# A hybrid decoder trunk: the decay gaps of the state space stage as one VectorE difference, clipped on ScalarE

## The reference, cut to what matters

```python
def step(state, inp):                      # one chunk, c = 128
    ...
    acum = jnp.cumsum(dtc * a.astype(jnp.float32), axis=1)
    diff = acum[:, :, None] - acum[:, None]            # (i, j, head)
    seg = jnp.exp(jnp.where(mask, diff, -jnp.inf))     # mask: j <= i
    xdt = xc * dtc[..., None]
    scores = jnp.einsum('bihn,bjhn->bijh', cc, bc) * seg
    y_intra = jnp.einsum('bijh,bjhp->bihp', scores, xdt)
    y_inter = jnp.einsum('bihn,bhpn->bihp', cc * jnp.exp(acum)[..., None], state)
    a_last = acum[:, -1]
    w = jnp.exp(a_last[:, None] - acum)[..., None]
    state = state * jnp.exp(a_last)[..., None, None] + jnp.einsum('bjhn,bjhp->bhpn', bc * w, xdt)
    return state, y_intra + y_inter
```

## Time and profile before

| | |
|---|---|
| median of 3 runs | 2202.1 us (2201.56 to 2203.22) |
| the profiled execution: its time | 2200.59 us |
| its span in the trace | 2198.8 us, so 1.8 us lie around the span |
| PE busy | 2137.9 us (97%) |
| DVE busy | 1230.1 us (56%) |
| ACT busy | 723.9 us (33%) |
| convolution stretch | 638 to 704 us in the span |
| chunk loop | 707 to 785 us in the span |

### The profile page before, as it was taken

How to read it: one execution, slowest core, us unless ns; L and a number is a source line. 1 busy time by engine, 2 the same in 40 slices (tenths; PEclk the granted TensorE clock), 3 DMA queues, 4 the chain that set the end, 5 groups by cost and what they waited for, 6 DMA issues and landing times.

```text
span 2198.8 us, 27851 instructions
## 1 busy us (share of the span) xinstructions
PE 2137.9 (97%) x10057; PEld 1738.0 (79%) x10057; DVE 1230.1 (56%) x1983; ACT 723.9 (33%) x1001; POOL 53.0 (2%) x94
## 2 busy tenths in 40 slices
PE   8999999999999989999999999999997999999998
PEld 7888888788787778888888888888755678888886
DVE  6535346586548986444356444445578545435344
ACT  4222224344325543222224222223355643222222
POOL 0000000000000000000000000000002300000000
PEclk9999999999999999999999999999998999999999
DMA  6333434322153324444443333333210013333321
GB/s 172 98 97 96 108 86 106 86 59 59 50 132 96 87 58 115 107 112 106 115 106 105 96 104 93 99 96 86 86 51 11 1 48 96 96 95 95 100 80 69
DMA packets 356347, 195.61 MB, mean 89 GB/s; under 512 B 13635, under 2 KB 348614, under 8 KB 356262
## 3 DMA queue, kind: packets, MB, share of 16 engines
q1 hardware_dynamic: 353622, 184.73, 29.7%
q0 software_dynamic: 2640, 9.77, 2.7%
HBM read 191.55 MB, written 2.79 MB: 88 GB/s over the span
## 4 chain that ended last, share of the span: by engine, by line
PE 86%; DVE 9%; issue 2%; ACT 2%; DMA 1%; POOL 0%; SPq 0%; DVEq 0%; ACTq 0%
PE ps L1435 25%; PE ps L1436 25%; PE ps L1437 25%; PE ps L1619 1%; PE ps L1904 1%; PE ps L1892 1%; DVE w_lo L786 1%; DVE index_scores L1318 1%; PE ps L1454 1%; PE ps L1455 1%; PE ps L1456 1%; PE ps L1636 1%; PE ps L1634 1%; PE ps L1635 1%; DVE index_scores L1303 1%
## 5 line engine op out<-in xcount | busy, mean ns | idle before, releaser
L467 ACT ACTIVATE w_hi<-w_raw 128x1024 fp32r<-128x1024 f32 x351 | 371.8, 1060 | 1067.6 <-PE ps L1437 994.7
L1435 PE MATMUL ps<-h_hi,w_hi 128*128 128x512 f32 x1640 | 641.4, 391 | 0.0
L1436 PE MATMUL ps<-h_lo,w_hi 128*128 128x512 f32 x1640 | 639.0, 390 | 0.0
L1437 PE MATMUL ps<-h_hi,w_lo 128*128 128x512 f32 x1640 | 638.9, 390 | 0.0
L786 DVE TENSOR_TENSOR w_lo<-w_raw,w_hi 128x1024 fp32r<-128x1024 f32 x351 | 429.0, 1222 | 290.5 <-ACT w_hi L467 290.4
L1435 PEld LDWEIGHTS ps<-h_hi,w_hi 128*128 128x128 f32 x1640 | 308.4, 188 | 66.0 <-issue 2.2
L1437 PEld LDWEIGHTS ps<-h_hi,w_lo 128*128 128x128 f32 x1640 | 308.4, 188 | 63.9
L1436 PEld LDWEIGHTS ps<-h_lo,w_hi 128*128 128x128 f32 x1640 | 308.5, 188 | 63.6
L1435 PE MATMUL ps<-act_hi,w_hi 128*128 128x512 f32 x704 | 274.0, 389 | 0.0
L1437 PE MATMUL ps<-act_hi,w_lo 128*128 128x512 f32 x704 | 273.9, 389 | 0.0
L1436 PE MATMUL ps<-act_lo,w_hi 128*128 128x512 f32 x704 | 273.9, 389 | 0.0
(11 more groups left out here) (301 smaller groups left out, 2086.3 us busy)
## 6 DMA issues: line engine op xcount, KB each, us to landing
w_raw<-in_ffn_w_gate SPq DMA_DIRECT2D x88, 512.0 KB, 3.8
w_raw<-in_ffn_w_up SPq DMA_DIRECT2D x88, 512.0 KB, 3.8
w_raw<-in_ffn_w_down SPq DMA_DIRECT2D x64, 512.0 KB, 3.9
w_raw<-in_hy_w_in SPq DMA_DIRECT2D x44, 512.0 KB, 3.8
w_raw<-in_ffn_w_down SPq DMA_DIRECT2D x32, 384.0 KB, 3.3
w_raw<-in_hy_w_out SPq DMA_DIRECT2D x16, 512.0 KB, 4.0
acum_rows<-acum_scratch POOLq DMA_DIRECT2D x4, 1024.0 KB, 9.9
bias_rows<-line_scratch POOLq DMA_DIRECT2D x8, 512.0 KB, 6.8
```

Source lines behind the costliest of these rows:

```text
L467: act.activation(w_hi[:, s, :], w_raw[:, s, :], ACT.Copy).then_inc(hi_ready, 1)
L1435: pe.matmul(ps[:, bank, :], wh, rh[:, k, :], start=k == 0, stop=False)
L1436: pe.matmul(ps[:, bank, :], wh, rl[:, k, :], start=False, stop=False)
L1437: mm = pe.matmul(ps[:, bank, :], wl, rh[:, k, :], start=False, stop=k == nk - 1)
```

## The change

DVE's 16 instructions of `gaps` become one TENSOR_TENSOR over 128 x 2048 elements, with the sign turned (`acum_j - acum_i`) and without the bound. ACT gets one more instruction over the same 128 x 2048, a Relu in place, which bounds the differences at zero from below, and a wait for it; the exponential then takes a scale of -1. Nothing else is changed.

```diff
@@ ACT, decays(c)
                     act.wait_ge(s_D, c + 1)
-                    act.activation(ssd_attn[:, c % 2, :, :], ssd_attn[:, c % 2, :, :], ACT.Exp).then_inc(s_pexp, 1)
+                    act.activation(ssd_attn[:, c % 2, :, :], ssd_attn[:, c % 2, :, :], ACT.Relu).then_inc(s_clip, 1)
+                    act.wait_ge(s_clip, c + 1)
+                    act.activation(ssd_attn[:, c % 2, :, :], ssd_attn[:, c % 2, :, :], ACT.Exp, scale=-1.0).then_inc(s_pexp, 1)
                     act.wait_ge(s_wd, c + 1)
@@ DVE, gaps(c)
-                    for h in range(SH):
-                        ins = dve.tensor_scalar(ssd_attn[:, c % 2, h, :], acum_chunk[:, h, :], acum_tok[:, c, h:h + 1], 0.0, ALU.subtract, ALU.min)
-                    ins.then_inc(s_D, 1)
+                    dve.tensor_tensor(ssd_attn[:, c % 2, :, :], acum_tok[:, c, :].rearrange("p (h o) -> p h o", o=1).to_broadcast([P, SH, P]),
+                                      acum_chunk, ALU.subtract).then_inc(s_D, 1)
```

More of the change, by code:

```diff
@@ L266, in build_program @@
         s_conv, s_conved, s_silu, s_pad = sem("s_conv"), sem("s_conved"), sem("s_silu"), sem("s_pad")
-        s_ea, s_pexp, s_wd, s_w, s_D, s_P, s_C = (sem(n) for n in ("s_ea", "s_pexp", "s_wd", "s_w", "s_D", "s_P", "s_C"))
+        s_ea, s_clip, s_pexp, s_wd, s_w, s_D, s_P, s_C = (sem(n) for n in ("s_ea", "s_clip", "s_pexp", "s_wd", "s_w", "s_D", "s_P", "s_C"))
         s_cbm, s_tr, s_trB, s_Bev, s_xdt, s_xdtw = (sem(n) for n in ("s_cbm", "s_tr", "s_trB", "s_Bev", "s_xdt", "s_xdtw"))
```

## The result

The changed kernel takes 2208.4 us (median of 20 runs, 2200.35 to 2211.84) against 2201.85 us before (20 runs, 2196.85 to 2203.54). The ratio is 1.0027, 95% interval 1.002 to 1.0034: slower by 0.2 to 0.34%. The profiled execution took 2207.52 us, its span is 2205.7.

What follows compares the result with a forecast made beforehand. DVE's chain through the last convolution tile and chunk loop was taken to bound the kernel, with PE behind it; 5.04 + 0.58 = +5.62 us gave a median of 2207.7 us, range 2206.7 to 2208.9, wider 2204.5 to 2210.5.

Steps and rivals of the forecast that it cites:

- DVE's gain: In gaps, one 2.28 us instruction replaces 16 taking 3.75, 3.23 and 3.22 us: 1.47, 0.95 and 0.94 us gained.
- ACT's price: Relu of 1.91 us before the exponential, table load no longer hidden: 3.23 us from Relu's start to exponential's start.
- The piece: From start of gaps to start of from_start, chunks 0 to 2: 9.66 us each, ACT the bound, together +5.04 us.
- the 2.58 us to spare on DVE: DVE's slack against ACT within each 9.66 us stretch from gaps to from_start, claimed for all three chunks.
- The convolution stretch: Before the chunk loop, the Relu beside chunk 0's decays makes the last convolution tile late by 0.58 us.
- The 0.29 us: Shorter gaps(0) lets DVE start the tile of m = 8 at 682.02, not 682.31, so ACT's following work starts earlier.
- Sum: Chunk loop 5.04 plus last convolution tile 0.58 us: +5.62 us, median from 2202.1 to 2207.7, +0.26%.
- The load doesn't hide: Rival, chance 0.10: the load hides behind the Relu, each of three pieces loses 1.30 us, leaving +1.7 us, not slower.
- part of the delay was swallowed: Rival, chance 0.16: engine hand-overs hide part, or the last tile's 0.58 is absent; +3.5 to +4.1 us, not slower.
- A dearer switch: Rival, chance 0.06 together with a dearer Relu: an undetected pipeline drain adds 1.3 us a piece, +9.6 us, 2211.7.
- PE's clock did fall: Rival, chance 0.06: PE's clock falls behind the longer wait for chunk 1's xdtw, adding 0 to 2 us, up to 2209.7.
- the 3.71: PE's forecast wait in us for xdtw of chunk 1: 1.96 before, with 1.75 more.

Runs made afterwards that it cites:

- e3: Changed kernel without the Relu, exponential scaled by -1/1024 (output not the reference's), so the DVE half alone: stretch -3.32 us against before, ratio 0.9989.
- e2: Kernel before, its 16 small DVE instructions kept, with only the Relu and the exponential of scale -1 added on ACT: stretch +8.75 us, ratio 1.0047.
- e1: Changed kernel plus a 128 x 1 exponential ahead of ACT's wait for the gaps, loading the set early: stretch +2.08 us against before, ratio 1.0013.
- e10: Changed kernel run again unaltered, with its trace: stretch 89.51 us, +5.62 against before, ratio 1.0027.
- e4: Changed kernel with ACT's exponentials for from_start and xdtw first, Relu and gaps' exponential last: stretch -3.28 us against before, ratio 0.9978.
- e7: Changed kernel with Relu and gaps' exponential last, and chunk 0's pair moved to just ahead of the chunk loop: stretch -4.63 us against before, ratio 0.9978.

## Why the prediction was right

**DVE's gain.** Forecast 2.28 us for the one difference; it took 2.28 to 2.29 in all four places, and e3 shows the gain alone, 1.47, 0.93 and 0.93 us. That the 1.47 comes out whole took the 3.75 us of the earlier trace rows, of which 0.53 is the long instruction of e2's section.

**ACT's price.** Forecast 1.91 for the Relu, 3.23 with the load; it took 1.90 to 1.94 and 3.21 to 3.25. That the load lies on the path was the larger point: e1 takes 3.57 us away by moving it ahead of the wait.

**The piece.** Forecast 9.66 in all three chunks, measured 9.66, 9.68, 9.67, so +5.07 where +5.04 was said. One reading in it was wrong without touching the sum: the 2.58 us to spare on DVE hold for chunks 1 and 2 (0.54 for PE and 1.89 for ACT, and 2.50). In chunk 0 DVE has 5.56, since its own work there was not 8.02 but 7.91 - 2.34 = 5.57 us before and is 4.1 now.

**The convolution stretch.** Forecast +0.58, measured +0.57. The 0.29 us that the shorter `gaps(0)` gives back are in it too: in e2, which lacks them, the tile is 0.86 late.

**Sum.** +5.62 forecast, +5.65 and +5.62 measured in the stretch. The medians moved by 6.55 us; for the changed kernel 2207.7 was forecast and 2208.4 measured. The further 0.9 us are not resolved: the stretch repeats to 0.03, the rest of an execution doesn't (816.1 to 819.3 us for one kernel in the part that e10 looks at), and the interval of the ratio (4.4 to 7.5 us) takes in both.

**The rivals.** The load doesn't hide: it starts 0.01 us after the Relu's end. No part of the delay was swallowed. A dearer switch isn't there: 1.31 us from the Relu's end to the exponential's start. PE's clock did fall, as that rival had it, but its price was nothing. PE's timeline in the changed kernel has 3.03 us of idle time ahead of chunk 1's `xdtw` matmuls, the first of which is in the earlier trace rows:

```profile
734.25 3.55 PE L1738 MATMUL ps<-xdtw,ssd_B 128*128 128x512 f32 x4 [3.03 <-DVE xdtw L1165]
```

The four took 1.95 us before, and the busy time by stretch shows the granted clock at about half, near 1.2 GHz, while they ran:

```profile
734.00:736.00 2.00, 1.75 (x2) 0.84 (x3) 2.00 (x3) 0.00 (x0) 0.00 (x0) 0.52 0.12 35
736.00:738.00 2.00, 2.00 (x7) 0.60 (x7) 2.00 (x2) 0.00 (x0) 0.00 (x0) 0.63 0.04 8
```

DVE waited 0.54 us for PE's outputs, and then still 1.89 for ACT: the late outputs used up DVE's spare time and no more. In e10 it came closer: 1.69 us for PE's outputs and then 0.72 for ACT, with the same piece of 9.67. So that this costs nothing is shown for two executions, with a margin of 0.72 us in one of them. The clock fell in a second place that the prediction doesn't name: the late tile makes PE wait 2.24 us for the last silu, ahead of the loop, instead of 1.68, and from 708 to 710 us the granted clock is 0.50 where it was 1.00. From the last tile to the first `gaps` of the loop DVE still takes 16.74 us in both kernels. The wait was 3.03 us and not the 3.71 that I worked out, since PE was done with the gate unit ahead of it only at 731.2; I took its end as unmoved but for the shift of the whole.

## What to carry to other kernels

Work that moves from one engine to another is priced by where the receiver's program puts it: behind the wait and ahead of what the other engine waits for, 1.9 us of Relu cost 1.9 us a piece; behind that, next to nothing in the loop (0.36 us in e4 and e7, for a weight half that came late). Look in the compiled order for what moves along: a first instruction that any function set can run pushes the load of the next set behind the wait, and one tiny instruction of that set ahead of the wait, or another order, brings it back (e1, e4). And where a kernel's executions spread more than the effect, compare one stretch between two events that the change doesn't touch.

## What the runs showed of the hardware that I had not expected

- The granted clock fell to 0.52 behind a wait of 3.03 us in the changed kernel, to 0.50 behind one of 4.10 us in e2, one of 2.42 us in e1 and one of 2.24 us in the changed kernel, and stayed at 1.00 behind the 1.96 us of the earlier trace rows; behind the same wait of 2.26 us in layer 1 it fell in one execution and not in another of the same kernel.
- A Relu doesn't bring a load of its own here, under the set of the silu (changed kernel) or of the exponential (e1, e4); e4 ran it behind the exponentials without one. The Trainium skill, "ScalarE: Activation LUTs", section "Table sets: the hidden batching unit", says that cheap functions are in every set, and the traces agree.
- An instruction that waits for the one ahead of it on ScalarE itself starts 0.03 us after its end (e4, 721.52 + 1.90 to 723.45), where one that doesn't wait starts 0.10 us before it (719.70 + 1.92 to 721.52): such a wait costs 0.13 us.
